# Even layer of a two-layer encoder step: VectorE operands from PSUM, and the second FFN's input parts made tile by tile

## The chip, the cores and the metric

The kernel runs on one core of a Trainium2 chip. The metric is the device time of one execution in microseconds (us). Every number below comes from the runs of the kernel before, from its profile or from its trace.

## The reference

One inference step of a two-layer encoder on 256 prompt rows and 64 sample rows of width 1024, in float32. The kernel treats both as 320 columns at once.

```python
def _trunk(x, past, prm):
    ...
    for i in range(DEPTH):
        h = _rmsnorm(x, prm['ffn_norm'][i, 0])
        x = x + 0.5 * _swiglu(h, ...)          # FFN 1 of the layer, D_FF = 2816
        h = _rmsnorm(x, prm['mix_norm'][i])
        mixed, ... = _mix_even(h, ...) if i % 2 == 0 else _mix_odd(h, ...)
        x = x + mixed
        h = _rmsnorm(x, prm['ffn_norm'][i, 1])
        x = x + 0.5 * _swiglu(h, ...)          # FFN 2 of the layer

def _mix_even(h, ...):
    q, k, v, qi, ki, wi, qb, kb, vb, rb, ab = _split(h @ w_in, EVEN_SIZES)
    q = _rmsnorm(q.reshape(bsz, L, A_HEADS, A_HEAD_DIM), q_norm)
    k = _rmsnorm(k.reshape(bsz, L, A_HEADS, A_HEAD_DIM), k_norm)
    ...
    o_a = _dsa_attention(q, k_all, v_all, qi, wi, ki_all, q_pos, k_pos, rel_bias, ...)
    log_alpha = jax.nn.log_sigmoid((ab @ gate_w2 + gate_b2)) / B_GATE_TAU
    o_b, s_new = _gla_chunked(qb, kb, vb, log_alpha, s0, min(CHUNK, L))
    o_b = _rmsnorm(o_b, gla_norm).reshape(bsz, L, B_VW) * jax.nn.silu(rb)
    out = jnp.concatenate([o_a.reshape(bsz, L, A_W), o_b], axis=-1) @ w_out
```

`_dsa_attention` picks the best k keys for each query by an indexer's score and attends to those; `_gla_chunked` takes a cumulative sum of `log_alpha` within chunks of 64 columns.

## The kernel before

Everything lies transposed: 128 partitions hold features, 320 columns hold tokens, and `xT`, the residual, is eight such tiles. Each large product is made of three: weights and inputs are split into a rounded high part and the rest as a low part (`h_hi`, `h_lo`, `w_parts`, `w_mix`, `ev_wo_hi`, `ev_wo_lo`), and TensorE adds high by high, high by low and low by high, three matmuls of 320 columns for each 128 x 128 block.

Each engine has its own program, written out in order, and runs it strictly in that order; semaphores with counts tie them together. So a wait holds all that stands behind it on its engine.

**The input projection of the even layer** (`even()` on TensorE, L770 to L780) makes 28 tiles of 128 features, two in each of 14 loads; tile t goes to PSUM bank t % 4. ScalarE makes the high part of each weight tile (`split_mix`, recorded at L1339), GpSimd the low part (L2619), and ScalarE and VectorE move finished tiles to `pr` in SBUF. Banks 4 to 7 are free for smaller products that stand between the loads: behind load 7 `head_sums` (L855) adds up the squares of q within each head, behind load 9 those of k, behind load 11 `gate()` (L861) makes the decay's argument. Before each of them TensorE waits until the banks are free (`qk_read` counts ScalarE's reads of the sums).

ScalarE makes 1/sqrt of these sums by Ln (L1374) and Exp (L1381), once for q behind load 8, once for k behind load 10, into `rs` and into `k_rstd`, a part of the weight buffer `dn`. Its softplus for the gate (L1556, L1557) stands behind load 12. VectorE in the meantime works through the top-k rounds (L2061, L2062), multiplies q by its norm (L2099, eight instructions, `q_ready`), goes on with five rounds of the top-k and the penalty, multiplies k (L2107, four, `k_ready`), adds the gate's bias (L2112, `gate_used`), and after ScalarE's softplus computes `gx` (L2117), its cumulative sums (L2121, ten scans) and two differences (L2124, L2126, `g_args`). Then it goes on with `logits` and `bds`. TensorE, with the projection behind it, does `scores(0)` to `scores(2)` (L938, banks 4 to 6), the token rows of v and k (L871) and the GLA products (L886 to L901). GpSimd follows its splits with `biased(1)`, `biased(2)` (L2653) and a scaling of `rb` (L2662).

**The output projection** (`project_out`, L698 to L700) makes eight tiles m of `xT`, two for each of four weight loads. The weight parts alternate between two buffers. TensorE's tile m waits for the low weight part of its pair (`wo_lo`) and for x of tile m - 2 (`x_upd`). ScalarE's order there is: `split_out(1)`, `split_out(2)` (waits for TensorE's tile 1), `split_out(3)` (waits for TensorE's tile 3), `split_gate_up(1, 0, 0, 0)`, the first weight tile of the next FFN, and then `ffn(1)`, which begins with the eight `h_hi`. VectorE's `residual` (L2003 to L2011) is:

```python
for m in range(KT):
    if m in (2, 4):
        split_out(base_dn, m // 2 + 1, wo, before)
    if m == 6:
        split(1 if base_dn == DN_EV else 3, gu, 0, 0, 0)
    ve.wait_ge((dn_half, dn_done)[m % 2], half_count(base_dn, m))
    tt(xT[:, m, :], bank(4 + m % 2, T), xT[:, m, :], ALU.add).then_inc(x_upd, 1)
```

GpSimd sums the squares of x tile by tile behind it (L2604 to L2607).

**The start of an FFN**: TensorE multiplies block k of the first weight tile as soon as `h_lo` of tile k is there (`h_ready`, L620 to L622); behind that first tile `norm` (L615) adds up the squares over the partitions. In FFN f = 2 (the first of the odd layer) ScalarE's `open_stage` makes `h_hi` of tile k as soon as x of tile k is there; in the other FFNs it waits for all eight, and VectorE's `low_parts` (L1907) makes the eight `h_lo` in one go in `ffn`.

Of the kernel before, what the change touches and what calls it, by code (L numbers as in the profile page):

```python
# [27 lines left out]
ALU = mybir.AluOpType  # L28
# [86 lines left out]
def build(nc, I, O):  # L115
    with ExitStack() as ctx:
# [84 lines left out]
        dwi = view(RA, 6400, 10, CH)  # L201
        k_rstd = dn[:, 1, 1280:2560].rearrange("p (a t) -> p a t", a=4)

# [143 lines left out]

        ev_o_hi = rounded("ev_o_hi", RB_at, KT, T)
        ev_o_lo = rounded("ev_o_lo", RB_at + T_QB * T, KT, T)
# [236 lines left out]
        def _(pe):  # L586
# [166 lines left out]
            def even():  # L753
                for l in range(len(EV_LOADS)):
                    project_in(GU_EV + l, 2 * l, h_lo_even)
                    if l == 0:
                        cached_keys(0)
                        cached_keys(1)
                    if l == 1:
                        key_token_rows()  # L760
                        cached_keys(2)
                        cached_keys(3)
                        cached_index_keys()
                    if l == 2:
                        raw_scores_x()
                    if l == 3:
                        combine_x()
                    if l == 4:
                        raw_scores_y()
                    if l == 5:  # L770
                        combine_y()
                    if l == 7:
                        head_sums(0, s["comb_used"], 2)
                    if l == 9:
                        head_sums(4, s["qk_read"], 1)
                    if l == 11:
                        gate()
                gla_and_attention()
                pe.wait_ge(s["l_done"], 8)
                pe.wait_ge(s["pt_evac"], 8)  # L780
                project_out(DN_EV, X_EV, ev_wo, 0, ev_o_hi, ev_o_lo, 4)
# [76 lines left out]
            def gate():  # L858
                pe.wait_ge(s["qk_read"], 2)
                for j in range(2):  # L860
                    ins = mm(bank(4 + j, T), w2[0:B_RANK, j * P:(j + 1) * P], pr[0:B_RANK, T_AB, :], start=True, stop=True)  # L861
                ins.then_inc(s["gate_pe"], 1)
# [11 lines left out]
            def gla_and_attention():  # L874
# [54 lines left out]
                def scores(b):  # L929
                    if b == 0:  # L930
                        pe.wait_ge(s["q_ready"], 8)
                        pe.wait_ge(s["k_ready"], 4)
                        pe.wait_ge(s["gate_used"], 1)
                    if b == 3:
# [393 lines left out]
        def _(sc):  # L1328
# [117 lines left out]
            def ffn(f, gain, x_base):  # L1446
# [5 lines left out]
                if f == 0:  # L1452
                    sc.wait_ge(pro_evac, 7)
                if f != 2:
                    sc.wait_ge(x_upd, x_base + 2)
                    for k in range(KT):
                        copy(h_hi[:, k, :], xT[:, k, :], cols[:, gain + k:gain + k + 1]).then_inc(h_hi_done, 1)
                        if f == 0 and k == 1:
                            split_gate_up(0, 0, 0, 0, (0,))
                else:  # L1460
                    open_stage(gain, x_base)
# [32 lines left out]
            def even():  # L1494
# [14 lines left out]
                for l, tiles in enumerate(EV_LOADS):  # L1509
# [35 lines left out]
                    if l == 8:  # L1545
                        sc.wait_ge(s["hsum"], 1)
                        for p in range(4):
                            act_(sqE[:, p, :], pr[:, T_K + p, :], ACT.Square).then_inc(s["hsq"], 1)
                        rsqrt(view(rs, 0, 4, T), banks(4, 4, T), 1.0 / A_D, (s["qk_read"], 1)).then_inc(s["qk_rstd"], 1)
                    if l == 10:  # L1550
                        sc.wait_ge(s["hsum"], 2)
                        rsqrt(k_rstd, banks(4, 4, T), 1.0 / A_D, (s["qk_read"], 2)).then_inc(s["qk_rstd"], 1)
                    if l == 12:
# [325 lines left out]
        def _(ve):  # L1879
# [30 lines left out]
            def ffn(f, gain):  # L1910
# [31 lines left out]
                if f == 0:  # L1942
# [9 lines left out]
                    ins.then_inc(first_total, 1)  # L1952
                elif f != 2:
                    low_parts(NORM_FFN[f], gain, range(KT))
# [49 lines left out]
            def residual(base_dn, wo, before):  # L2004
                for m in range(KT):
# [4 lines left out]
                    ve.wait_ge((dn_half, dn_done)[m % 2], half_count(base_dn, m))  # L2010
                    tt(xT[:, m, :], bank(4 + m % 2, T), xT[:, m, :], ALU.add).then_inc(x_upd, 1)  # L2011

            def half_count(base_dn, m):
# [4 lines left out]
            def even():  # L2018
# [77 lines left out]
                for p in range(A_PAIRS):  # L2096
                    for par in range(2):
                        h = slice(par * A_D, (par + 1) * A_D)
                        ins = stt(qbd[h, :, p, par * CH:(par + 1) * CH],  # L2099
                                  pr[h, T_Q + p, :].rearrange("p (c t) -> p c t", t=CH)[:, :, ::-1], cols[h, C_QN:C_QN + 1],  # L2100
                                  rs[h, p * T:(p + 1) * T].rearrange("p (c t) -> p c t", t=CH)[:, :, ::-1], ALU.mult, ALU.mult)
                        ins.then_inc(s["q_ready"], 1)
# [3 lines left out]
                for p in range(A_PAIRS):  # L2106
                    stt(pr[:, T_K + p, :], pr[:, T_K + p, :], cols[:, C_KN:C_KN + 1], k_rstd[:, p, :],  # L2107
                        ALU.mult, ALU.mult).then_inc(s["k_ready"], 1)
# [7 lines left out]
                ve.wait_ge(s["g_ln"], 1)  # L2116
                link(stt(gx, gx, 0.0, gx2, ALU.min, ALU.subtract))  # L2117
                for p in range(B_PAIRS):
                    for c in range(NCH):
                        w = slice(c * CH, (c + 1) * CH)  # L2120
                        ins = ve.tensor_tensor_scan(gB[:, p, w], ones[:, 0:CH], gx[:, p, w], 0.0, ALU.mult, ALU.add)  # L2121
                link(ins)
# [666 lines left out]
```

## Time and profile before

| | us |
|---|---|
| median of 3 runs | 1477.51 |
| lowest and highest | 1476.26 and 1480.02 |
| the profiled execution | 1478.12 |
| its span, first to last instruction | 1476.4 |
| TensorE matmul busy | 1423.6 (96%) |
| VectorE busy | 896.6 (61%) |
| ScalarE busy | 597.5 (40%) |
| GpSimd busy | 370.6 (25%) |

The mean granted clock of TensorE is 0.979 of full. In the profile, times are counted from the span's start; "[5.30 <-DVE RB L2192]" behind an instruction says that its engine had been idle for 5.30 us and what ended that. Lines of helpers stand for many places: L1339 is every copy of ScalarE, L1907 every `h_lo`. PE is TensorE, DVE VectorE, ACT ScalarE and POOL GpSimd. PS is the PSUM. "PEclk" is the granted clock as a share of 2.4 GHz. Matmuls overlap, so their durations are longer than their spacing.

### The profile page before, as it was taken

To read this page: it belongs to the slowest core of one execution; us is meant where nothing else is said; L and a number is where in the kernel's file an instruction comes from. 1 tells how busy PE (TensorE), PEld (TensorE's weight loads), DVE (VectorE), ACT (ScalarE), POOL (GpSimd) and SP (SyncE) were. 2 spreads that over 40 slices of the span, in tenths; PEclk is the share of its full clock that TensorE was granted. 3 is DMA by queue.
4 is the path that set the end of the run, shared out by engine and by line. 5 is a ranking of instruction groups with operands and counts; after the bars stand their busy time and mean duration, and the time that the engine had idled before them with its cause. 6 is when DMAs were issued, how large, how long until landed. Compare 5 with 4: busy or idle time off the path is not lost.

```text
span 1476.4 us, 25253 instructions
## 1 busy us (share of the span) xinstructions
PE 1423.6 (96%) x9708; PEld 1389.8 (94%) x9708; DVE 896.6 (61%) x1403; ACT 597.5 (40%) x975; POOL 370.6 (25%) x344
## 2 busy tenths in 40 slices
PE   7999999999779999999999999999999889999998
PEld 7999999999658999999999999989999779999998
DVE  5666655678755666655666655667565456666542
ACT  5333324446443433332433332558433544333322
POOL 4000024766415100012100003637766232000000
PEclk9999999999789999999999999989999999999999
DMA  7655951344202555864455684122222222555751
GB/s 186 179 158 146 285 146 42 116 129 139 87 3 87 143 144 157 210 178 97 123 158 145 167 228 117 58 86 87 59 85 58 90 85 82 155 157 147 185 149 44
DMA packets 324028, 188.23 MB, mean 127 GB/s; under 512 B 10954, under 2 KB 321352, under 8 KB 323964
## 3 DMA queue, kind: packets, MB, share of 16 engines
q1 hardware_dynamic: 322080, 183.22, 45.0%
q0 software_dynamic: 1216, 3.98, 0.9%
q8 instruction: 43, 0.70, 0.2%
q10 hardware_dynamic: 668, 0.15, 0.1%
q14 instruction: 21, 0.17, 0.0%
HBM read 183.22 MB, written 4.11 MB: 127 GB/s over the span
## 4 chain that ended last, share of the span: by engine, by line
PE 89%; DVE 6%; ACT 3%; issue 1%; DMA 1%; SPq 0%; ACTq 0%
PE PS L620 21%; PE PS L621 21%; PE PS L622 21%; PE PS L725 2%; PE PS L726 2%; PE PS L727 2%; PE PS L1193 2%; PE PS L1176 2%; PE PS L746 1%; PE PS L748 1%; PE PS L747 1%; PE PS L698 1%; PE PS L699 1%; PE PS L700 1%; DVE RA L2099 1%
## 5 line engine op out<-in xcount | busy, mean ns | idle before, releaser
L620 PE MATMUL PS<-h_hi,w_parts 128*128 128x320 f32 x1408 | 438.2, 311 | 7.1 <-DVE h_lo L1907 4.1
L621 PE MATMUL PS<-h_lo,w_parts 128*128 128x320 f32 x1408 | 436.4, 310 | 0.0
L622 PE MATMUL PS<-h_hi,w_parts 128*128 128x320 f32 x1408 | 436.3, 310 | 0.0
L620 PEld LDWEIGHTS PS<-h_hi,w_parts 128*128 128x128 f32 x1408 | 265.5, 189 | 8.8 <-issue 7.4
L621 PEld LDWEIGHTS PS<-h_lo,w_parts 128*128 128x128 f32 x1408 | 265.5, 189 | 0.3
L622 PEld LDWEIGHTS PS<-h_hi,w_parts 128*128 128x128 f32 x1408 | 265.4, 189 | 0.0
L1339 ACT ACTIVATE w_parts<-gu 128x1024 fp32r<-128x1024 f32 x176 | 176.6, 1050 | 158.4 <-PE PS L622 154.8
L620 PE MATMUL PS<-act_hi,w_parts 128*128 128x320 f32 x704 | 217.7, 309 | 0.0
L622 PE MATMUL PS<-act_hi,w_parts 128*128 128x320 f32 x704 | 217.6, 309 | 0.0
L621 PE MATMUL PS<-act_lo,w_parts 128*128 128x320 f32 x704 | 217.6, 309 | 0.0
L1895 DVE TENSOR_TENSOR w_parts<-gu,w_parts 128x1024 fp32r<-128x1024 f32 x176 | 209.1, 1229 | 3.4 <-ACT w_parts L1339 3.3
L2619 POOL TENSOR_TENSOR w_mix<-gu,w_mix 128x512 fp32r<-128x512 f32 x116 | 154.5, 1345 | 107.7 <-ACT w_mix L1339 107.5
L1339 ACT ACTIVATE w_parts<-dn 128x1408 fp32r<-128x1408 f32 x64 | 84.8, 1373 | 183.5 <-PE PS L622 183.5
L621 PEld LDWEIGHTS PS<-act_lo,w_parts 128*128 128x128 f32 x704 | 132.2, 188 | 0.0
L620 PEld LDWEIGHTS PS<-act_hi,w_parts 128*128 128x128 f32 x704 | 132.1, 188 | 0.0
L622 PEld LDWEIGHTS PS<-act_hi,w_parts 128*128 128x128 f32 x704 | 132.1, 188 | 0.0
L2607 POOL TENSOR_TENSOR RB<-xT 128x320 f32<-128x320 f32 x5 | 3.6, 719 | 485.2 <-DVE xT L1939 472.2
L1450 ACT ACTIVATE rs<-rs 128x320 f32<-128x320 f32 x88 | 41.5, 472 | 204.6 <-DVE rs L1920 204.6
L1895 DVE TENSOR_TENSOR w_parts<-dn,w_parts 128x1408 fp32r<-128x1408 f32 x64 | 118.8, 1896 | 7.2 <-ACT w_parts L1339 7.1
L1926 DVE TENSOR_TENSOR rs<-rs,PS 128x320 f32<-128x320 f32 x88 | 42.9, 487 | 127.2 <-PE PS L622 126.8
L1339 ACT ACTIVATE w_mix<-gu 128x512 fp32r<-128x512 f32 x116 | 71.7, 629 | 117.6 <-PE PS L727 64.9
L1935 DVE TENSOR_TENSOR rs<-PS,RB 128x320 f32<-128x320 f32 x32 | 15.7, 491 | 137.7 <-PE PS L622 137.7
(386 smaller groups left out, 2380.5 us busy)
## 6 DMA issues: line engine op xcount, KB each, us to landing
gu<-in_ffn_w_gate SPq DMA_DIRECT2D x88, 512.0 KB, 4.0
gu<-in_ffn_w_up SPq DMA_DIRECT2D x88, 512.0 KB, 5.2
dn<-in_ffn_w_down SPq DMA_DIRECT2D x32, 1408.0 KB, 7.0
gu<-in_od_w_in SPq DMA_DIRECT2D x32, 512.0 KB, 5.0
gu<-in_ev_w_in SPq DMA_DIRECT2D x26, 512.0 KB, 4.8
dn<-in_ev_w_out SPq DMA_DIRECT2D x4, 1024.0 KB, 6.3
dn<-in_od_w_out SPq DMA_DIRECT2D x4, 1024.0 KB, 5.4
RB<-bias_rows POOLq DMA_DIRECT2D x2, 576.0 KB, 6.1
```

Source lines behind the costliest of these rows:

```text
L620: mm(out, w_hi, hi, start=first, stop=False)
L621: mm(out, w_hi, lo, start=False, stop=False)
L622: return mm(out, w_lo, hi, start=False, stop=last)
L725: mm(out, w_hi, h_hi[:, k, :], start=(k == 0), stop=False)
L726: mm(out, w_hi, h_lo[:, k, :], start=False, stop=False)
L727: ins = mm(out, w_lo, h_hi[:, k, :], start=False, stop=(k == KT - 1))
L1176: ins = mm(bank(4)[:, p * P:(p + 1) * P], level[:, c, p, :], uT[:, c, p, :], start=True, stop=True)
L1339: return act_(out, in_, ACT.Copy, scale=scale)
L1450: act_(tanh_g[:, slot, :], gated[:, slot, :], ACT.Tanh, scale=0.5).then_inc(tanh_done, 1)
L1895: tt(w_parts[:, slot, 1, w], raw[:, slot, w], w_parts[:, slot, 0, w].bitcast(F32), ALU.subtract)\
L1926: tt(gated[:, slot, :], gated[:, slot, :], bank(2 * slot + 1, T), ALU.mult).then_inc(act_done, 1)
L2619: po.tensor_tensor(mix_parts(n, t)[:, 1, w].rearrange("p (k c) -> p k c", k=4), raw[:, 4 * half:4 * half + 4, :], mix_parts(n, t)[:, 0, w] ...
```

## The change

In the even layer's input projection ScalarE writes the two norms, of q and of k, back into PSUM banks 4 to 7, in place of the sums, and VectorE reads them there. `gx` behind the softplus goes to banks 4 and 5, and the scans read it there. Since the banks are in use for longer, three waits of TensorE change: the second `head_sums` waits for `q_ready`, `gate()` for `k_ready`, and `scores(0)` for `g_args` instead of `gate_used`.

In the output projection of the even layer VectorE makes `h_lo` of tile m - 1 behind x of tile m, and the last one behind the loop; ScalarE makes `h_hi` by `open_stage`, tile by tile, in FFN 2 of the even layer (f = 1) too. The order of ScalarE's program is as before. `ev_o_hi` moves to another place in RB, since `h_lo` is now written while it is read. The odd layer is untouched.

```diff
-        k_rstd = dn[:, 1, 1280:2560].rearrange("p (a t) -> p a t", a=4)
...
-        ev_o_hi = rounded("ev_o_hi", RB_at, KT, T)
+        ev_o_hi = rounded("ev_o_hi", RB_at + T_V * T, KT, T)
...
                     if l == 9:
-                        head_sums(4, s["qk_read"], 1)
+                        head_sums(4, s["q_ready"], 8)
...
             def gate():
-                pe.wait_ge(s["qk_read"], 2)
+                pe.wait_ge(s["k_ready"], 4)
...
                     if b == 0:
                         pe.wait_ge(s["q_ready"], 8)
                         pe.wait_ge(s["k_ready"], 4)
-                        pe.wait_ge(s["gate_used"], 1)
+                        pe.wait_ge(s["g_args"], 1)
...
-                if f != 2:
+                if f in (0, 3):
                     sc.wait_ge(x_upd, x_base + 2)
...
-                        rsqrt(view(rs, 0, 4, T), banks(4, 4, T), 1.0 / A_D, (s["qk_read"], 1)).then_inc(s["qk_rstd"], 1)
+                        rsqrt(banks(4, 4, T), banks(4, 4, T), 1.0 / A_D, (s["qk_read"], 1)).then_inc(s["qk_rstd"], 1)
...
-                        rsqrt(k_rstd, banks(4, 4, T), 1.0 / A_D, (s["qk_read"], 2)).then_inc(s["qk_rstd"], 1)
+                        rsqrt(banks(4, 4, T), banks(4, 4, T), 1.0 / A_D, (s["qk_read"], 2)).then_inc(s["qk_rstd"], 1)
...
-                elif f != 2:
+                elif f == 3:
                     low_parts(NORM_FFN[f], gain, range(KT))
...
                     ve.wait_ge((dn_half, dn_done)[m % 2], half_count(base_dn, m))
                     tt(xT[:, m, :], bank(4 + m % 2, T), xT[:, m, :], ALU.add).then_inc(x_upd, 1)
+                    if base_dn == DN_EV and m:
+                        low_parts(NORM_FFN[1], C_FFN + 8, (m - 1,))
+                if base_dn == DN_EV:
+                    low_parts(NORM_FFN[1], C_FFN + 8, (KT - 1,))
...
-                                  rs[h, p * T:(p + 1) * T].rearrange("p (c t) -> p c t", t=CH)[:, :, ::-1], ALU.mult, ALU.mult)
+                                  bank(4 + p, T)[h, :].rearrange("p (c t) -> p c t", t=CH)[:, :, ::-1], ALU.mult, ALU.mult)
...
-                    stt(pr[:, T_K + p, :], pr[:, T_K + p, :], cols[:, C_KN:C_KN + 1], k_rstd[:, p, :],
+                    stt(pr[:, T_K + p, :], pr[:, T_K + p, :], cols[:, C_KN:C_KN + 1], bank(4 + p, T),
                         ALU.mult, ALU.mult).then_inc(s["k_ready"], 1)
...
-                link(stt(gx, gx, 0.0, gx2, ALU.min, ALU.subtract))
+                link(stt(banks(4, 2, T), gx, 0.0, gx2, ALU.min, ALU.subtract))
...
-                        ins = ve.tensor_tensor_scan(gB[:, p, w], ones[:, 0:CH], gx[:, p, w], 0.0, ALU.mult, ALU.add)
+                        ins = ve.tensor_tensor_scan(gB[:, p, w], ones[:, 0:CH], bank(4 + p, T)[:, w], 0.0, ALU.mult, ALU.add)
```

## Rows read from the trace of the kernel before

**Rows 1.** The page's chain of work that ended last, shares of the span by engine.

```profile
PE 89%; DVE 6%; ACT 3%; issue 1%; DMA 1%; SPq 0%; ACTq 0%
```

**Rows 2.** VectorE in order of time: start, us, line, operation, tiles, shapes, count, [idle before].

```profile
330.01 0.49 DVE L2024 TENSOR_TENSOR RB<-PS,RB 128x320 f32<-128x320 f32 x1
334.75 11.21 DVE L2099 SCALAR_TENSOR_TENSOR RA<-RB,cols,rs 64x320 f32<-64x320 f32 x8 [4.25 <-ACT rs L1381]
...
356.44 5.99 DVE L2107 SCALAR_TENSOR_TENSOR RB<-RB,cols,dn 128x320 f32<-128x320 f32 x4
...
367.07 1.56 DVE L2117 SCALAR_TENSOR_TENSOR RA<-RA 128x640 f32<-128x640 f32 x1 [2.86 <-ACT RA L1557]
368.66 6.08 DVE L2121 TENSOR_TENSOR_SCAN RA<-ones,RA 128x64 f32<-128x64 f32 x10
...
375.51 0.82 DVE L2126 TENSOR_TENSOR rs<-RA 128x640 f32<-128x640 f32 x1
...
391.83 0.82 DVE L2144 TENSOR_TENSOR RB<-PS,RB 64x640 f32<-64x640 f32 x1 [3.37 <-PE PS L894]
```

**Rows 3.** GpSimd in order of time, the same stretch.

```profile
335.31 11.81 POOL L2619 TENSOR_TENSOR w_mix<-gu,w_mix 128x512 fp32r<-128x512 f32 x8 [6.21 <-ACT w_mix L1339]
...
366.67 3.62 POOL L2653 TENSOR_TENSOR RB<-RB 128x512 f32<-128x512 f32 x2 [4.58 <-PE PS L748]
370.25 2.88 POOL L2662 TENSOR_TENSOR RB<-RB 128x1280 f32<-128x1280 f32 x1
```

**Rows 4.** ScalarE in order of time, the same stretch.

```profile
333.44 1.27 ACT L1381 ACTIVATE rs<-rs 128x1280 f32<-128x1280 f32 x1
...
348.96 1.27 ACT L1381 ACTIVATE dn<-dn 128x1280 f32<-128x1280 f32 x1
...
360.12 0.42 ACT L1339 ACTIVATE RB<-PS 128x320 f32<-128x320 f32 x1
364.24 0.74 ACT L1556 ACTIVATE RA<-RA 128x640 f32<-128x640 f32 x1 [3.71 <-DVE RA L2115]
```

**Rows 5.** TensorE in order of time, the same stretch.

```profile
334.17 2.32 PE L855 MATMUL PS<-RA,RB 128*128 128x320 f32 x8
...
350.98 1.34 PE L861 MATMUL PS<-RB 16*128 16x320 f32 x4
...
366.42 3.25 PE L938 MATMUL PS<-RB,RA 128*128 128x64 f32 x24
...
376.72 2.32 PE L871 MATMUL PS<-ident,RB 128*128 128x128 f32 x8 [5.30 <-DVE RB L2192]
```

**Rows 6.** Busy time and granted clock in short stretches: PE, PEld, DVE, ACT, POOL, then PEclk.

```profile
428.00:429.00 1.00, 0.00 (x0) 0.00 (x0) 0.93 (x4) 0.17 (x2) 0.00 (x0) 0.50 0.00 0
...
445.00:446.00 1.00, 1.00 (x6) 1.00 (x5) 1.00 (x2) 0.32 (x1) 0.00 (x0) 0.51 0.86 268
...
448.00:449.00 1.00, 1.00 (x7) 1.00 (x7) 0.00 (x0) 0.00 (x0) 0.00 (x0) 0.78 0.46 123
```

**Rows 7.** ScalarE in order of time, output projection and start of FFN 2.

```profile
459.87 2.01 ACT L1339 ACTIVATE ev_wo_hi<-dn 128x1024 fp32r<-128x1024 f32 x2 [5.03 <-PE PS L700]
461.78 1.99 ACT L1339 ACTIVATE w_parts<-gu 128x1024 fp32r<-128x1024 f32 x2
474.42 3.73 ACT L1339 ACTIVATE h_hi<-xT,cols 128x320 fp32r<-128x320 f32 x8 [10.65 <-DVE xT L2011]
```

**Rows 8.** VectorE in order of time, the same stretch.

```profile
445.05 2.47 DVE L2001 TENSOR_TENSOR ev_wo_lo<-dn,ev_wo_hi 128x1024 fp32r<-128x1024 f32 x2
...
459.81 0.49 DVE L2011 TENSOR_TENSOR xT<-PS,xT 128x320 f32<-128x320 f32 x1 [2.37 <-PE PS L700]
...
475.01 4.54 DVE L1907 SCALAR_TENSOR_TENSOR h_lo<-xT,cols,h_hi 128x320 fp32r<-128x320 f32 x8 [0.63 <-ACT h_hi L1339]
```

**Rows 9.** TensorE in order of time, the same stretch.

```profile
475.74 0.39 PE L620 MATMUL PS<-h_hi,w_parts 128*128 128x320 f32 x1 [1.89 <-DVE h_lo L1907]
...
483.67 0.70 PE L615 MATMUL PS<-RB,ones 128*128 128x320 f32 x2
```

## The prediction

> **What bounds the kernel now.** I read the page's chain of work first. TensorE holds 89% of it, VectorE 6%, ScalarE 3% [rows 1]: time can only come from the places where TensorE stands still or runs at the lower of its two clocks (1.2 instead of 2.4 GHz), and anything that makes it stand still anew costs in full. The change touches two such places, so I read the engines in order of time there.
>
> The first is the end of the even layer's input projection. VectorE computes q (L2099), ends the top-k rounds, then k (L2107), the gate and the scans (L2121), while TensorE goes on projecting [rows 2, 5]. The eight instructions of q take 11.21 us, 1.4 us each, and the four of k 5.99 us, though a multiply of the same 320 columns with one operand in PSUM takes 0.49 us in the same stretch (L2024) [rows 2]. GpSimd runs its splits at 11.81 / 8 = 1.48 us each beside them [rows 3]: VectorE advances at GpSimd's pace. The scans show it again: ten take 6.08 us, and the last eight fit between the end of GpSimd's L2662 (373.13) and 374.77, 0.2 us each [rows 2, 3]. TensorE ends the projection at 366.42, does scores and value rows, and then stands 5.30 us until g_args (376.33) and the first logits let it on [rows 2, 5].
>
> The second place is the step from the output projection to FFN 2. TensorE ends tile 7 at 475.74 - 1.89 = 473.85, and its first weight tile of FFN 2 ends at 483.67 [rows 9]. Its 48 products take 7.04 us at 14.1 us for 96 (352.3 to 366.42, four projection tiles) [rows 5], so 9.82 - 7.04 = 2.8 us are lost there: ScalarE starts the eight h_hi only when all of x is there, VectorE the eight h_lo behind them [rows 7, 8].
>
> **Front part: q, k and gate operands in PSUM.** q: rstd is ready at 334.71 [rows 4]; 8 x 0.49 = 3.9 us give q at 338.7 instead of 346.0. The bounds are 0.49 us (L2024, one PSUM operand) and 1.4 us (L2099 itself) [rows 2]; I take the first, since L2024 ran beside the same GpSimd work. k: 4 x 0.49 = 2.0 us instead of 5.99.
> But the banks are now held. TensorE's second head_sums waited for qk_read (the Ln, two activations before the end of rstd) and did not stand; now it waits for the last q. It is there at 334.17 [rows 5] and starts at 338.8: **4.6 us idle**, with the projection tiles 20 to 27 queued behind it. ScalarE's evacuations and GpSimd's splits follow TensorE's tiles, so they move by 4.6 too: k's rstd comes at 350.23 + 4.6 = 354.8 [rows 4] (VectorE, which took 10.5 us from the end of q to L2107 [rows 2], is there at 349.2 and waits for it), k at 356.8. TensorE reaches gate() at 350.98 + 4.6 = 355.6 and waits until 356.9, 1.3 us more. The projection ends 5.9 us later, at 372.3.
> The gate chain follows ScalarE, whose place for it lies behind tile 25: 360.54 + 5.9 = 366.4. Exp, table and Ln took from 364.24 to 367.07, 2.8 us [rows 2, 4]: 369.25. L2117 keeps two SBUF inputs, but GpSimd is idle until 372.5, so 0.8 us instead of 1.56 (L2126, same 640 columns, is the low bound) [rows 2]: 370.1. Scans 10 x 0.2 = 2.0: 372.1. Two subtractions, 1.56 us, the second of which meets GpSimd's biased(1), now at 372.5: 0.9 us more, g_args at 374.6. That is 376.33 - 374.6 = **-1.7 us**.
> After it: scores(0) used to be done in the shadow and now waits for g_args; 8 of 24 matmuls of 3.25 us [rows 5] plus the semaphore, **+1.2 us**, with VectorE's logits(0) and everything behind them waiting. Bounds: 0 (other work ends last) and 3.4 (all three scores).
> Clock: the output projection starts behind a stop and thin work, and its granted clock was 0.51 from 445 and 0.78 in the microsecond from 448, some 3.4 us at half rate [rows 6]; in another stop (PE busy 0.00) it was down at 428 [rows 6]. I take the same 3.4 us behind the new 4.6 us stop, in which half the work gets done: **+1.7 us**, bounds 0 and 3.4. In return TensorE no longer stands 5.3 us before the attention: it works on almost without a stop from g_args, likely at the higher clock, and VectorE's wait of 3.37 us for the GLA scores (L2144) [rows 2] shrinks. I take 2.4 of the 3.37: **-2.4 us**, bounds 0 and -3.4.
> GpSimd's biased(2) and the scaling of rb (3.62 + 2.88 us with biased(1) [rows 3]) now run beside bds(), which has two SBUF inputs: up to 2.9 us, in the range only. Sum of the front: -1.7 + 1.2 + 1.7 - 2.4 = **-1.2 us**, from -4.5 to +3.
>
> What the notes say against it: the Trainium skill (VectorE: DVE Perf Modes, section on the TRN2 errata) gives a VectorE instruction from PSUM 62 cycles more fixed time than from SBUF; by it q and k would cost some 12 x 0.065 = 0.8 us more, an estimate by that page. L2024 with its PSUM operand at 0.49 us against 1.4 for L2099 shows that here the wait for GpSimd outweighs it. The Trainium skill (SBUF — State Buffer, section "SBUF: two separate sides") says that an instruction with two SBUF inputs is blocked whole by a GpSimd one that reads SBUF. By it L2117, whose output alone moves to PSUM, stays exposed.
>
> **Back part: h_hi and h_lo of FFN 2 inside the output projection.** TensorE can start FFN 2 at once; h_lo of tiles 0 to 6 is ready, that of tile 7 is needed 3.1 us later and takes 0.49 + 0.59 + 0.57 us. Gain **-2.8 us**, all that was lost.
> What is queued behind the new waits decides, though. VectorE waits for h_hi of tile 0 right behind its x of tile 1, **in front of** split_out(2), which makes the low weights of tiles 4 and 5. ScalarE makes that h_hi behind split_out(2), split_out(3) and FFN 2's first gate_up split, and split_out(3) waits for TensorE's tile 3: it starts at 459.87, the gate_up split ends at 461.78 + 1.99 = 463.77 [rows 7]. Then h_hi 0.59 (464.4), h_lo 0.57 (464.95) [rows 7, 8], the two halves of split_out(2) 2.47 (467.4), x of tile 2 0.49 (467.95) [rows 8], and only then may TensorE start tile 4. It was through with tile 3 at 459.8 [rows 8] and did not stop before. **+8.2 us** of idle, and it falls to the lower clock: +1.7 us as above, bounds 1.5 and 3.4. From there VectorE keeps up: split_out(3) is done at some 472.6, tile 4 ends at 473.2, tile 6 starts at 476.7, tile 7 ends at 483.8. GpSimd's squares follow x and hide as before; SP's queue has nothing moved. Moving ev_o_hi costs nothing.
> Sum of the back: 8.2 + 1.7 - 2.8 = **+7.1 us**, from +5.5 to +9.
>
> **Sum.** -1.2 + 7.1 = +5.9 us. The profiled execution took 1478.12 us (span 1476.4), 0.6 above the median of 1477.51; carried to the median: 1477.5 + 5.9 = **1483.4 us**. About 0.3% (4.4 us) is what a measurement of this kernel can tell from no change, so below 1473.1 is faster and above 1481.9 slower.
>
> **Rivals.**
> (B) The front keeps more: the clock stays up in the 4.6 us stop and VectorE finds no GpSimd work. Front -4, sum +3.1: 1480.6, no change. For it: behind the 1.89 us stop before FFN 2 the 48 products leave no room for 3.4 us at half rate [rows 9]. Against: in the stop around 428 it was down before TensorE went on [rows 6]. Chance 0.21.
> (C) The front loses: bds() behind GpSimd (+2.9), all scores ahead of the logits and no return of the clock. Front +3: 1477.5 + 3 + 7.1 = 1487.6. Chance 0.09.
> (D) The other side: VectorE's new wait costs nothing, since h_hi of tile 0 comes in time. The point: it must be there by 459.8 - 0.49 - 2.47 - 0.57 = 456.3, where ScalarE's order gives 464.4. Then the back is -2.8 and the front -1.2 to -2.9: 1473.5 to 1471.8. Only another order on ScalarE would do it. Chance 0.05.
> (E) The change does not do what it says: PSUM operands leave VectorE at GpSimd's pace. Then q ends at 346, head_sums waits 11.9 us instead of 4.6, k takes 6: front +8, 1477.5 + 8 + 7.1 = 1492.6. L2024 speaks against it. Chance 0.04.
>
> **How the numbers follow.** My forecast, (A), has 0.61; its own range is 1481 to 1487, with 0.08 of its chance below 1481.9. Slower: 0.53 + 0.09 + 0.04 = 0.66. No change: 0.08 + 0.21 + 0.02 = 0.31. Faster: 0.03. The range 1479.0 to 1488.5 takes in (A), (B) and (C).
>
> **What the changed profile would show.** L2099 at about 0.5 us each beside GpSimd's splits (E if 1.4). TensorE idle about 4.6 us before L855, released by VectorE, and 1.3 before L861; clock 0.5 behind it (B if not). Scans near 2 us in all; g_args some 1.7 us earlier. In the output projection VectorE idle about 11 us before L1907 of tile 0, released by ScalarE, and TensorE about 8 us before L698 of tile 4; no stop before FFN 2's L620. The prediction is wrong if TensorE runs through tile 4, if the clock after either stop stays full, or if the return in the attention is absent or above 3.4 us.

## The result and the profile after

The changed kernel takes 1488.52 us (median of 4 executions, 1487.96 to 1488.99), the kernel before in the same series 1478.57 (1476.26 to 1480.02). The ratio is 1.0074, with an interval from 1.0062 to 1.0086: **+10.9 us** on 1477.5, where the prediction had +5.9. The direction was right, the size was not; the time lies 5 us above the forecast of 1483.4 and 0.02 us above the upper end of the range, 1488.5. The profiled execution of the changed kernel took 1487.96 us (span 1486.2).

Two stretches carry it. I lay the two traces over each other at the last norm product ahead of the change (TensorE's sum over `total`, 253.49 us before, 253.13 after), so 0.36 us is added to the times of after when they are set against times of before.

| from there, us | before | after | difference | forecast |
|---|---|---|---|---|
| g_args ready | 122.84 | 124.45 | +1.6 | -1.7, +1.7 for the clock |
| output projection starts | 190.43 | 194.23 | +3.8 | -1.2 |
| first norm product of FFN 2 | 230.18 | 241.36 | +11.2 | +5.9 |
| output projection alone | 39.75 | 47.13 | +7.4 | +7.1 |

The back came out as forecast; the front was missed by 5 us. Which waits are new for TensorE is seen in the view of waits (what waited, for whom, us in total, times, longest). After:

```profile
PE PS L697 <- DVE xT L2010: 8.0, 1, 8.0
...
PE PS L854 <- DVE RA L2102: 5.0, 1, 5.0
...
PE PS L937 <- DVE rs L2129: 2.2, 1, 2.2
...
PE PS L860 <- DVE RB L2110: 1.2, 1, 1.2
```

All four were in the prediction: 8.2 us before tile 4 of the output projection (L697), 4.6 before the second head_sums (L854), 1.3 before gate() (L860), and, without a length, the scores behind g_args (L937).

**VectorE, front, after** (start, us, then line, operation and operands; what answers to [rows 2]):

```profile
334.32 4.60 DVE L2102 SCALAR_TENSOR_TENSOR RA<-RB,cols,PS 64x320 f32<-64x320 f32 x8 [4.15 <-ACT PS L1380]
...
356.37 1.93 DVE L2110 SCALAR_TENSOR_TENSOR RB<-RB,cols,PS 128x320 f32<-128x320 f32 x4 [7.23 <-ACT PS L1380]
...
372.16 0.83 DVE L2120 SCALAR_TENSOR_TENSOR PS<-RA 128x640 f32<-128x640 f32 x1 [9.63 <-ACT RA L1556]
373.03 1.89 DVE L2124 TENSOR_TENSOR_SCAN RA<-ones,PS 128x64 f32<-128x64 f32 x10
...
375.69 1.89 DVE L2129 TENSOR_TENSOR rs<-RA 128x640 f32<-128x640 f32 x1
...
379.76 2.41 DVE L2199 TENSOR_SCALAR RB<-RB 128x4 f32<-128x4 f32 x1
...
395.05 1.66 DVE L2147 TENSOR_TENSOR RB<-PS,RB 64x640 f32<-64x640 f32 x2 [1.76 <-PE PS L893]
```

q takes 4.60 us instead of 11.21, k 1.93 instead of 5.99, the scans 1.89 instead of 6.08 [rows 2]. One line is odd: L2199 works on four elements per partition and takes 2.41 us; the same line takes 0.17 at 383.51. GpSimd says why:

```profile
375.58 3.69 POOL L2656 TENSOR_TENSOR RB<-RB 128x512 f32<-128x512 f32 x2 [5.09 <-PE PS L747]
379.23 2.91 POOL L2665 TENSOR_TENSOR RB<-RB 128x1280 f32<-128x1280 f32 x1
```

Its scaling of rb runs from 379.23 to 382.14, and L2199 ends when it does (382.17). Before, this scaling was over at 373.13, ahead of the logits [rows 3].

**TensorE, front, after**, and its clock in the windows that hold the two stops (window; length, busy us; granted clock, 1.00 is 2.4 GHz and 0.50 is 1.2; DMA):

```profile
338.98 4.11 PE L854 MATMUL PS<-RA,RB 128*128 128x320 f32 x8 [4.97 <-DVE RA L2102]
358.35 1.34 PE L860 MATMUL PS<-RB 16*128 16x320 f32 x4 [1.18 <-DVE RB L2110]
```

```profile
334.00:339.00 5.00, 0.03 (x2) 1.00 0.00 0
339.00:343.00 4.00, 4.00 (x9) 0.57 0.42 123
355.00:359.00 4.00, 2.82 (x18) 1.00 0.48 170
359.00:363.00 4.00, 4.00 (x16) 0.60 0.01 2
```

The clock falls twice: behind the stop of 4.97 us (head_sums takes 4.11 us, against 2.32 before), and again at 359, right behind the stop of only 1.18 us. In both stretches together TensorE worked for 6.8 us at the lower clock. The prediction had one fall here.

**The step to FFN 2, after** (TensorE, then VectorE, then ScalarE; the counterpart of [rows 7 to 9]):

```profile
447.36 0.38 PE L697 MATMUL PS<-ev_o_hi,ev_wo_hi 128*128 128x320 f32 x1 [1.83 <-issue]
471.19 0.61 PE L697 MATMUL PS<-ev_o_hi,ev_wo_hi 128*128 128x320 f32 x1 [7.97 <-DVE xT L2010]
494.49 0.70 PE L614 MATMUL PS<-RB,ones 128*128 128x320 f32 x2
```

```profile
467.69 0.55 DVE L1906 SCALAR_TENSOR_TENSOR h_lo<-xT,cols,h_hi 128x320 fp32r<-128x320 f32 x1 [10.99 <-ACT h_hi L1338]
468.16 2.48 DVE L2000 TENSOR_TENSOR ev_wo_lo<-dn,ev_wo_hi 128x1024 fp32r<-128x1024 f32 x2
470.55 0.48 DVE L2010 TENSOR_TENSOR xT<-PS,xT 128x320 f32<-128x320 f32 x1
```

```profile
465.22 1.98 ACT L1338 ACTIVATE w_parts<-gu 128x1024 fp32r<-128x1024 f32 x2
467.11 1.00 ACT L1338 ACTIVATE h_hi<-xT,cols 128x320 fp32r<-128x320 f32 x2
```

This is the chain as forecast. VectorE stands 10.99 us for h_hi of tile 0, which ScalarE makes behind its gate_up split; then the split of the weights of tiles 4 and 5, then x of tile 2, then tile 4, with TensorE idle for 7.97 us.

### The profile page after: what moved, and what is told of

Its sections match the earlier page's. It is cut to its first block, busy times and chain, and to the rows that moved or that the text cites. A ratio compares the mean times of both kernels' runs of the same rounds, so it can differ in the third digit from the quotient of the medians.

```text
span 1486.2 us, 25253 instructions
## 1 busy us (share of the span) xinstructions
PE 1424.8 (96%) x9708; PEld 1391.6 (94%) x9708; DVE 885.9 (60%) x1403; ACT 597.9 (40%) x975; POOL 367.9 (25%) x344
## 3 DMA queue, kind: packets, MB, share of 16 engines
HBM read 183.22 MB, written 4.11 MB: 126 GB/s over the span
## 4 chain that ended last, share of the span: by engine, by line
PE 90%; ACT 4%; DVE 4%; issue 1%; DMA 0%; ACTq 0%; DVEq 0%
PE PS L619 21%; PE PS L621 21%; PE PS L620 21%; PE PS L724 2%; PE PS L725 2%; PE PS L726 2%; PE PS L745 2%; PE PS L747 2%; PE PS L746 2%; PE PS L1192 2%; PE PS L1175 2%; PE PS L697 1%; PE PS L698 1%; PE PS L699 1%; DVE RA L2309 1%
```

## The experiments

Differences in us are the ratio to the kernel before, less one, times 1477.5; the brackets hold the 95% interval. The ratio compares means and the totals given are medians, so the two can differ by a us or two. One execution differs from another of the same kernel by up to some 7 us (all_good from 1471.9 to 1478.7), at times with a different mean granted clock. Each kernel has one trace, so where two executions of it part is not shown; across the kernels, TensorE's work at the lower clock between 378 and 450 us goes from 14.3 us (g_only) to 27.4 (shifted). A single trace is therefore exact for its durations and not for the total.

**The two parts alone.** First the back, without the operands in PSUM:

```diff
-        ev_o_hi = rounded("ev_o_hi", RB_at, KT, T)
+        ev_o_hi = rounded("ev_o_hi", RB_at + T_V * T, KT, T)
...
-                if f != 2:
+                if f in (0, 3):
...
+                    if base_dn == DN_EV and m:
+                        low_parts(NORM_FFN[1], C_FFN + 8, (m - 1,))
...
```

> Only the output projection's part of the change (h_hi and h_lo tile by tile, ev_o_hi moved); the projection and the gate as before. Theory 1, the two parts are separate and the back costs what the changed trace shows, 7.4 us: 1478 + 7.4 = about 1485, with TensorE idle 8.0 us before tile 4 of the output projection and a granted clock of 0.5 behind that stop. Theory 2, the 3.8 us that the changed kernel had lost before the output projection belong to the moved ev_o_hi and not to the PSUM operands: 1489, and TensorE begins the output projection 3.8 us late here too. As predicted blind: +7.1.

Measured: 1483.9 us, **+6.2** [4.1, 8.3]. As the first theory said: the back alone loses. Its output projection begins no later than before (188.3 us from the norm product, 190.4 before), so the moved ev_o_hi is not the front's loss, and the stop before tile 4 is 7.97 us, as in the changed kernel:

```profile
442.32 0.39 PE L698 MATMUL PS<-ev_o_hi,ev_wo_hi 128*128 128x320 f32 x1 [1.84 <-issue]
466.14 0.61 PE L698 MATMUL PS<-ev_o_hi,ev_wo_hi 128*128 128x320 f32 x1 [7.97 <-DVE xT L2011]
```

Then the front, with the back left as it was (`head_sums` behind `q_ready`, `gate()` behind `k_ready`, rsqrt in place in the banks, gate and scans from PSUM, scores behind `g_args`):

> Only the PSUM operands with their three waits; the output projection as before. Theory 1: +3.8 us, about 1482, with stops of TensorE of 5.0 us before the second head_sums and 1.2 us before gate(), the clock at 0.5 behind each, and the output projection beginning 3.8 us late. Theory 2: within 1 us of the kernel before. As predicted blind: -1.2.

Measured: 1481.9 us, **+3.5** [2.1, 5.0]. The two parts sum to +9.7, the whole measured +10.9 [9.2, 12.7]: they add. The front was forecast at -1.2 and is where the prediction failed.

**The back with the wait moved.** If the back's loss is the wait of VectorE ahead of split_out(2), then making h_lo of tiles 0 to 3 only behind x of tile 4 must remove it and leave the gain at the start of FFN 2:

```diff
-                    if base_dn == DN_EV and m:
-                        low_parts(NORM_FFN[1], C_FFN + 8, (m - 1,))
+                    if base_dn == DN_EV and m >= 4:
+                        low_parts(NORM_FFN[1], C_FFN + 8, range(4) if m == 4 else (m - 1,))
```

> The back part with another order on VectorE: the h_lo of tiles 0 to 3 only behind x of tile 4 (so behind split_out(3)), then one behind each x. No front part. If the whole loss of the back is VectorE's wait for h_hi of tile 0 in front of split_out(2): TensorE doesn't stop in the output projection, FFN 2 starts at once, -2.8 us against the kernel before, about 1475.7. If the low parts themselves or their traffic cost something there: no faster than before, or TensorE stops before tile 5 or 6.

Measured: 1473.47 us, **-3.8** [-5.5, -2.2]. VectorE's rows show both splits of the weights now ahead of the first h_lo, each waiting 0.73 us at most:

```profile
453.33 3.05 DVE L2001 TENSOR_TENSOR ev_wo_lo<-dn,ev_wo_hi 128x1024 fp32r<-128x1024 f32 x2 [0.73 <-ACT ev_wo_hi L1339]
...
460.37 3.05 DVE L2001 TENSOR_TENSOR ev_wo_lo<-dn,ev_wo_hi 128x1024 fp32r<-128x1024 f32 x2 [0.73 <-ACT ev_wo_hi L1339]
463.75 3.02 DVE L1907 SCALAR_TENSOR_TENSOR h_lo<-xT,cols,h_hi 128x320 fp32r<-128x320 f32 x4
```

From the start of the output projection (443.27) to FFN 2's norm product (480.08) it takes 36.8 us, against 39.75 before: -2.9 where the forecast had -2.8 for this gain. The total gained more, 3.8, with an interval that takes in 2.9. VectorE's wait and the clock behind it were the whole loss of the back.

**The front taken apart.** q alone (rstd of q in PSUM, head_sums behind q_ready), then the gate alone (gx and scans in PSUM, scores behind g_args), then q with k, then q with the gate:

> Only q's norm in PSUM, with the second head_sums behind q_ready; k, gate and scans as before. Theory 1, TensorE's stop before the second head_sums is the main cost: idle 5.0 us there, some 3.4 us at a granted clock of 0.5 behind it, the projection ends 6.5 us later than before and without a second stop before gate(). The kernel is slower than before by 0 to +3 us, since the scans then meet less of GpSimd. Theory 2, the stop costs nothing in the end because the attention waits for VectorE's chain anyway: within 0.5 us of before.

> Only gx and the scans in PSUM, with scores(0) behind g_args; q and k as before. The scans should take 1.9 us instead of 6.08, and g_args come 1.5 us earlier (the two subtractions still wait for GpSimd's scaling of rb). TensorE then stands some 8 us before scores(0) and works at 0.5 behind that; logits(0) begins 1.2 us behind g_args. If the wait of the scores is what eats the scans' gain: 0 to +2 us against before. If not: -1.5.

> q's and k's norms in PSUM with the two waits of the second head_sums and of gate(); gate and scans in SBUF, scores(0) behind gate_used as before. Known so far: q alone is 1.8 us faster than before, gx and the scans alone 1.3 us faster, all three together 3.7 us slower. Theory 1, the second stop of TensorE (1.2 us before gate()) and the second stretch at a clock of 0.5 behind it are what turns the sum: this one is 2 to 4 us slower than q alone, so 1478 to 1480. Theory 2, it is the wait of the scores for g_args, on a chain that the first stop has already delayed: this one is as fast as q alone, about 1476.

> q's norm and the gate with the scans in PSUM, k in SBUF; gate() doesn't wait for k. Theory 1 (the second stop): close to q alone, 1475 to 1477. Theory 2 (the scores' wait behind the delayed chain): 2 to 4 us slower than q alone, 1478 to 1480.

| kernel | us | against before | new stops in the projection | g_args, from the norm product (before: 122.84) |
|---|---|---|---|---|
| q_only | 1476.12 | -1.8 [-3.1, -0.3] | 4.97 | 121.63 |
| g_only | 1476.62 | -1.6 [-3.1, -0.3] | none | 121.05 |
| q_and_k | 1481.68 | +2.8 [+1.0, +4.6] | 4.98, 1.18 | 124.36 |
| q_and_g | 1478.85 | +1.3 [-0.1, +2.8] | 4.97 | 122.18 |
| front_only | 1481.90 | +3.5 [+2.1, +5.0] | 4.97, 1.18 | 124.91 |

The expectation for q alone fell under either theory: the long stop and the clock behind it cost less than the faster q gives back. The gate alone came out at its second case, -1.5: TensorE stands 8.09 us before its scores and does them at the lower clock (6.31 us instead of 3.25), as expected, and still the gain of g_args is kept. q_and_k went in the direction of the second stop, and further than expected (1481.7 against 1478 to 1480): k costs 4.6 us on top of q, though its four instructions are 4 us shorter. What k adds for TensorE is the short stop:

```profile
338.66 3.97 PE L854 MATMUL PS<-RA,RB 128*128 128x320 f32 x8 [4.98 <-DVE RA L2098]
357.89 1.55 PE L860 MATMUL PS<-RB 16*128 16x320 f32 x4 [1.18 <-DVE RB L2106]
```

But this doesn't show that the short stop costs the 4.6 us. q_and_k's executions fall into two groups, four from 1476.5 to 1477.4 us at a mean clock of 0.977 to 0.980 and six from 1481.5 to 1482.4 at 0.973 to 0.976. The trace is from the faster group (1477.13), and it has both stops and both half-rate stretches (6.4 us of work at the lower clock from 326 to 378). So an execution with both is no slower than before; what divides the two groups isn't shown, since no trace of the slower one was kept.

q and the gate, each worth 1.6 to 1.8 us, give nothing together. q_and_g has no second stop, so the first theory put it at 1475 to 1477; it came out where the second did, 1478 to 1480, the one in which the scores' wait for g_args stands on a chain that the first stop has delayed. From g_args to the first GLA mask it takes 17.1 us, q_only 15.6: the first scores are waited for 1.26 us, which q_only doesn't. GpSimd's scaling of rb, the work that L2199 met above, isn't the difference: q_and_g pays it in one piece (2.39 us for the first logits' small instruction) and q_only in two (0.89 and 1.52 for the first and the second), where g_only has 0.17.

**Is it the clock?** Two tests. The first moves head_sums behind load 10 and gate() behind load 12, so that q is done in time (ScalarE's norm of k moves one load back with them):

```diff
-                    if l == 9:
+                    if l == 10:
                         head_sums(4, s["q_ready"], 8)
-                    if l == 11:
+                    if l == 12:
                         gate()
```

> q's and k's norms in PSUM, but the second head_sums and gate() one load of the projection later (behind loads 10 and 12), so that TensorE finds the banks free; gate and scans as before. If the front's loss is TensorE's two stops and the clock behind them: no stop in the projection, clock 1.00 throughout it, the projection ends when it did before, and the softplus starts 2 us earlier, -1 to -2.5 us against before. If PSUM operands cost something of their own: no gain.

Measured, for q and k together: 1475.29 us, **-2.5** [-4.0, -1.0], instead of +2.8 unmoved. The time is as expected, the way to it is not, since the projection was to have no stop. The stops have changed places as well as shrunk: head_sums used to cover a wait for GpSimd's split of the next weights, which now stands open, and the short stop stays.

```profile
335.94 0.38 PE L745 MATMUL PS<-h_hi,w_mix 128*128 128x320 f32 x1 [2.32 <-POOL w_mix L2618]
360.61 1.34 PE L860 MATMUL PS<-RB 16*128 16x320 f32 x4 [1.18 <-DVE RB L2106]
```

So this run alone doesn't divide stop from clock. The second test does: front_only with both stops kept and filled with products that nobody reads (fed_first has only the first line):

```diff
             def head_sums(squares_before, free, n_free):
+                for _ in range(20 if squares_before else 0):
+                    mm(bank(0)[:, 320:448], ones[:, :], ones[:, :], start=True, stop=True)
                 pe.wait_ge(free, n_free)
...
             def gate():
+                for _ in range(4):
+                    mm(bank(0)[:, 320:448], ones[:, :], ones[:, :], start=True, stop=True)
                 pe.wait_ge(s["k_ready"], 4)
```

> The front part alone, with TensorE's two new stops filled: 20 products of 128 x 128 ahead of the wait for the last q, 4 ahead of the wait for the last k. They go into unused columns of bank 0 and nobody reads them; each should take 0.21 us, so both waits still end when VectorE is ready. Theory 1 (the clock is what the front loses): front_only had 7.77 us of TensorE's busy time at the lower clock from 326 to 378, the kernel before 0.92; half of the difference, 3.4 us, comes back, and the time is 1478 to 1479 against 1477.8 before. Theory 2 (the stops and the later work behind them are the loss): 1481 to 1482.5, as front_only.

> As front_fed, with only the first stop (20 products) filled; the stop of 1.2 us before gate() is left empty. If the clock falls a second time only because this short stop comes soon behind the long one, nothing falls now and the time is that of front_fed. If the short stop brings it down by itself, TensorE runs some 3.4 us at the lower clock behind it: 1.7 us more than front_fed, 1480 to 1481.

Measured: front_fed 1477.65 us, **+0.3** [-1.0, +1.6]; fed_first 1477.63, **0.0** [-1.3, +1.3]. This is the first theory's case, a little better even. Doing useless work in the stops gives back the 3.3 to 3.5 us that lie between these and front_only; in the traces g_args comes 3.7 us earlier (121.24 from the norm product in both, 124.91 in front_only). TensorE's rows of front_fed: the filling takes 4.63 us, and head_sums 2.42 us instead of 4.11.

```profile
334.38 4.63 PE L852 MATMUL PS<-ones 128*128 128x128 f32 x40
339.52 2.42 PE L856 MATMUL PS<-RA,RB 128*128 128x320 f32 x8 [0.51 <-DVE RA L2102]
```

In fed_first the short stop is there, 1.19 us, and the clock stays up behind it:

```profile
356.61 1.34 PE L862 MATMUL PS<-RB 16*128 16x320 f32 x4 [1.19 <-DVE RB L2108]
```

```profile
339.00:343.00 4.00, 4.00 (x21) 1.00 0.50 126
355.00:359.00 4.00, 2.81 (x14) 1.00 0.03 9
359.00:363.00 4.00, 4.00 (x30) 1.00 0.38 109
```

So with the first stop filled, the short one doesn't bring the clock down. In the changed kernel, where it comes 18 us behind the end of the first stop, it did (0.60 in 359:363). That a half-rate stretch must lie before it doesn't follow, though: in shifted the clock is full behind the stop of 2.32 us that ends at 335.94, and falls all the same behind the short one.

```profile
336.00:337.00 1.00, 1.00 (x7) 1.00 0.00 0
363.00:364.00 1.00, 1.00 (x6) 0.50 0.00 0
```

**GpSimd's meeting with the logits.** front_wait is front_only with GpSimd's scaling of rb held until the third logits' maximum is there, so that L2199 is free:

```diff
             po.wait_ge(*evacuated(N_EV - 1))
+            po.wait_ge(s["nmx"], 3)
             po.tensor_tensor(pr[:, T_RB
```

> The front part alone, with GpSimd's scaling of rb made to wait until VectorE has done the third logits. If the 2.41 us of the first logits' small tensor_scalar (4 elements) are GpSimd's scaling beside it: that instruction takes 0.17 us, VectorE reaches the GLA operands 2.2 us earlier, and the kernel is 1.0 to 2.2 us faster than front_only. If it is a wait for something else, or TensorE and ScalarE set that time anyway: same as front_only within 0.5 us.

Measured: 1481.46 us, **+3.4** [2.1, 4.9], no gain over front_only. L2199's counterpart takes 0.17 us, but the scaling now meets bds() (4.49 us for four instead of 1.79) and TensorE waits 2.84 us there instead. The run doesn't price the meeting, it moves it:

```profile
385.37 3.01 POOL L2662 TENSOR_TENSOR RB<-RB 128x1280 f32<-128x1280 f32 x1 [6.22 <-DVE RB L2195]
```

```profile
385.14 4.49 DVE L2133 SCALAR_TENSOR_TENSOR RB<-RB,RA 64x320 f32<-64x320 f32 x4
```

pool_order puts it behind all of bds(), in the kernel before, and biased(2) behind g_args:

```diff
             biased(1)
+            po.wait_ge(s["g_args"], 1)
             biased(2)
             po.wait_ge(*evacuated(N_EV - 1))
+            po.wait_ge(s["bds_ready"], 3)
```

> The kernel before with another order on GpSimd alone: biased(2) waits for g_args and the scaling of rb for the last bds(). No operand moves to PSUM and TensorE's waits are as before. If the scans' 6.08 us are only GpSimd's work beside them, L2117 and the scans take 2.7 us together instead of 7.7, g_args come about 4 us earlier, and the kernel is 2 to 4 us faster. If the time behind g_args is set by ScalarE or by TensorE's clock: less than 1 us.

Measured: 1474.22 us, **-3.0** [-4.9, -1.0], inside what was expected, without a single operand moved to PSUM. (L2117 still meets biased(1) and takes 1.57 us, so it and the scans take 3.5 us together, not 2.7.) The ten scans, with both inputs in SBUF, take 1.93 us (6.08 before [rows 2]; 1.89 from PSUM), and g_args comes 4.1 us earlier than before. It was GpSimd that made them slow, not SBUF:

```profile
369.11 1.93 DVE L2121 TENSOR_TENSOR_SCAN RA<-ones,RA 128x64 f32<-128x64 f32 x10
...
371.82 0.82 DVE L2126 TENSOR_TENSOR rs<-RA 128x640 f32<-128x640 f32 x1
```

**What can be had.** late_low and pool_order together; the same with q in PSUM and its stop filled; the same with q and k shifted; and that with the short stop filled:

> The two faster versions together: h_lo of tiles 0 to 3 behind x of tile 4, and GpSimd's biased(2) and scaling of rb later; no operand in PSUM. They touch separate stretches, so their gains should add: -4.7 - 3.0, about 1470.5.

> late_and_pool with q's part of the change (rstd of q in PSUM, head_sums behind the last q) and 20 idle products in the stop of 5 us. q alone gained 1.8 us with 3.2 us at the lower clock, which costs 1.6. Theory 1: up to 3.4 us below late_and_pool (1470.6), 1467 to 1469. Theory 2, or if GpSimd's new order already gives what q's part gives: 1470 to 1471.

> late_and_pool and the shifted PSUM norms of q and k (second head_sums behind load 10, gate() behind load 12). If shifted's gain of 2.5 us is its own: 1 to 2.5 us faster than late_and_pool, 1468 to 1469.5. If it is the same as the GpSimd order's (both only bring g_args forward): no faster than late_and_pool.

> The kernel all_good (late h_lo, GpSimd's order, q and k in PSUM with head_sums and gate() one load later) with 5 idle products ahead of gate()'s wait. all_good had 6.6 us of busy time at the lower clock from 326 to 378. Theory 1: with the clock kept up it comes to 1477.3 - 3 = 1474, and if q and k then pay as they do alone, to 1469 to 1471. Theory 2: 1477 as before.

| kernel | us | against before | g_args, from the norm product |
|---|---|---|---|
| late_and_pool | 1470.64 | -6.1 [-7.8, -4.4] | 118.72 |
| late_pool_q_fed | 1472.22 | -4.7 [-6.5, -3.0] | 120.03 |
| all_good | 1477.29 | -1.5 [-3.4, +0.4] | 121.85 |
| best_fed | 1477.64 | -1.0 [-2.7, +0.4] | 121.90 |

The first is the best version: both gains add within their intervals (-3.8 and -3.0), as expected, and it beats both kernels. q in PSUM gives nothing on top of it, even with its stop filled, and came out above both of its cases: GpSimd's new order already gives what q's part gave, and head_sums still waits for the last q, so g_args comes 1.3 us later. all_good is the second case of its expectation, no faster than late_and_pool, and slower than that says. best_fed came out at its second theory's 1477 and not at the first's 1474 or less, although the filling of the short stop does hold the clock up behind it (3.35 us of TensorE's work at the lower clock from 326 to 378 instead of 6.6). The 1.6 us that this should be worth are within the spread of both kernels. Its other stop, 2.32 us behind GpSimd's split of the weights, stays open, with the clock at 0.50 behind it.

Why all_good is slower than late_and_pool, by 4.6 us in the ratios and 6.7 in the medians, while shifted is 2.5 us faster than before, is not settled: g_args comes 3.1 us later, and the rest is open.

## Why the prediction was wrong in size

**The back, right.** Idle 7.97 us (8.2 forecast). The clock stays at 0.50 until close to 476 (0.58 in the microsecond from 475), with 4.65 us of TensorE's work in it, which costs 2.3 us (1.7 forecast):

```profile
466.00:471.00 5.00, 0.00 (x0) 0.00 (x0) 3.28 (x5) 2.11 (x4) 0.00 (x0) 0.50 0.00 0
471.00:475.00 4.00, 3.81 (x14) 3.85 (x15) 3.96 (x6) 1.12 (x2) 3.58 (x4) 0.50 0.01 4
475.00:479.00 4.00, 4.00 (x26) 4.00 (x26) 1.84 (x3) 0.56 (x1) 2.83 (x3) 0.89 0.00 0
```

The start of FFN 2 gives 2.9 back (2.8 forecast). Sum +7.4, in the trace +7.4, forecast +7.1. late_low confirms the cause: it moves only VectorE's place for h_lo, and the whole loss is gone.

**The front, wrong by 5 us.** front_fed, which has the front without the clock's part, lets each term be read. From g_args (374.90) to the first GLA mask (L2147 at 392.35) its trace has 17.45 us, the kernel before 15.50 (376.33 to 391.83 [rows 2]). The second to the fourth term make up that difference of 1.95 but for 0.05:

| term of the sum | forecast | measured | from |
|---|---|---|---|
| g_args without the clock | -1.7 | -1.6 | 122.84 and 121.24 from the norm product |
| scores(0) behind g_args | +1.2 | +1.3 | VectorE waits 1.26 us for the first scores |
| L2199 behind the scaling of rb | 0 (range) | +2.2 | 2.40 us instead of 0.17 |
| wait for the GLA scores shrinks | -2.4 | -1.6 | 1.76 us instead of 3.37 |
| clock in the projection | +1.7 | +3.3 to 3.5 | front_only less front_fed and fed_first |
| sum | -1.2 | +3.6 to 3.8 | front_only: +3.5 |

The rows behind the third and the fourth term, in front_fed:

```profile
376.16 0.42 DVE L2195 TENSOR_TENSOR RB<-PS,RB 128x256 f32<-128x256 f32 x1 [1.26 <-PE PS L941]
...
377.07 2.40 DVE L2199 TENSOR_SCALAR RB<-RB 128x4 f32<-128x4 f32 x1
...
392.35 1.66 DVE L2147 TENSOR_TENSOR RB<-PS,RB 64x640 f32<-64x640 f32 x2 [1.76 <-PE PS L897]
```

Three steps failed, then, by 1.6 to 1.8, 2.2 and 0.8 us:

1. **"I take the same 3.4 us behind the new 4.6 us stop" counted one fall of the clock.** The stop before gate() stood in the prediction with 1.3 us, and was priced as idle time alone. It came with a second half-rate stretch, as dear as the first (3.4 us of work at the lower clock in each, in the changed kernel). Each stretch at the forecast's 1.7 us makes 3.4; the filled stops measure 3.3 to 3.5. The price of one stretch was right, their number was not.
2. **The meeting of the scaling with VectorE was put "in the range only", as up to 2.9 us beside bds().** It came, 2.2 us, beside the logits. The prediction looked at instructions with two SBUF inputs; L2199 has one, and is tiny. But it is blocked whole: it ends with GpSimd's instruction. The Trainium skill (SBUF — State Buffer, section "SBUF: two separate sides") names, beside instructions with two SBUF inputs, those in a two-port performance mode as taking the port pair that VectorE shares with GpSimd. The trace agrees that this one is blocked (2.41 and 2.40 us against 0.17), while L2195 and L2198 beside the same GpSimd work were not held; in which mode it ran the trace doesn't show.
3. **The return of 2.4 us was 1.6.** The attention behind g_args is not bound by TensorE's clock alone. It still has stops of 1.7 and 1.8 us there, for ScalarE's evacuations, and its GLA scores run at half rate as before (4.37 us for L893, as for L894 before):

```profile
385.41 1.31 PE L878 MATMUL PS<-ident,RB 128*128 128x128 f32 x10 [1.73 <-ACT RB L1338]
388.48 2.37 PE L885 MATMUL PS<-ident,RB 128*128 128x128 f32 x10 [1.76 <-ACT RB L1338]
390.64 4.37 PE L893 MATMUL PS<-RB 128*128 128x64 f32 x20
```

**Two things that the prediction had wrong beside its terms.** Its bounds don't add up to its range. From -1.7 with bounds of 0 and 3.4 for the scores, 0 and 3.4 for the clock and 0 and -3.4 for the return, the front goes from -5.1 to +5.1, and to +8.0 with the 2.9 of the meeting; it was given as -4.5 to +3, which leaves out the +3.6 to +3.8 that came. By the same terms (C) is a front of +6.3 and not +3, and 1490.9 instead of 1487.6. And the choice of 0.49 us for q and k rested on L2024 having run "beside the same GpSimd work". It hadn't: it ran from 330.01 to 330.50, and GpSimd was idle for the 6.21 us before 335.31 [rows 3]. That q came out at 0.54 to 0.56 us each, with GpSimd's splits beside it from 334.90 on, was therefore lucky as to its reason; only the changed kernel shows it.

**The rivals.** (C), the front at +3 with no return and a meeting with GpSimd, was nearest as a number (1487.6), though its mechanism was only half right and its sum was off: the meeting came at another instruction, part of the return came too, and the second fall of the clock was in no case. (E) fell: q at 0.54 to 0.56 us each, k at 0.48. (D) was named as needing "another order on ScalarE"; late_low shows that another order on VectorE is enough, since h_lo of tiles 0 to 3 is needed by nobody before FFN 2. (B) fell with the clock. The warning about slower PSUM operands came to nothing: ten scans take 1.89 us from PSUM and 1.93 from SBUF.

## What to carry to other kernels

Price a stop of the bounding engine with its clock, and a short stop as well: behind one of 1.2 us the clock fell for a stretch that cost 1.7. Give that term a chance, since it doesn't come behind every stop of that length. When two engines slow each other, first try to move the other engine's work (here two waits on GpSimd, -3.0 us) before moving operands, because an operand that is also a bank somebody waits for buys its speed with a new wait. Work that is pulled forward "tile by tile" belongs behind the last thing that the bounding engine needs from that queue, not at the first moment at which its input exists.

## What of the hardware was not expected

- The length of a stop doesn't tell whether TensorE's clock falls behind it. Behind 1.18 us it fell in the changed kernel (0.60 in 359:363) and in shifted, and behind 1.19 us it stayed at 1.00 in fed_first. Behind 2.32 us it stayed at 1.00 in shifted and fell in best_fed. The stop of 1.89 us before FFN 2 left it at 1.00 in the kernel before and brought it to 0.50 in front_fed; the two rows are of front_fed and of before, in this order. What decides, the runs don't show.

```profile
477.00:478.00 1.00, 1.00 (x4) 0.50 0.02 8
477.00:478.00 1.00, 1.00 (x8) 1.00 0.00 0
```

- Products of 128 x 128 that nobody reads, at 0.23 us each, 20 of them in a stop of 5 us, were worth 3.5 us of a kernel of 1478 (fed_first against front_only).
- A VectorE instruction on 128 x 4 elements took 2.40 us instead of 0.17 beside a GpSimd instruction of 2.91 us.
